# Reordering the first mixer layer of a one-core encoder kernel: q/k products, one output-gate tile and the gate logits ahead of the S5 input matrices

## What is computed

```
proj = xn @ w_in                       # 1024 -> 4 x 512: u, xm, v, o_pre
y_a = s5_group(u)                      # 32 groups x 16 channels, 64 complex states each
xc = silu(conv4(xm))                   # per head of 128
q, k = xc @ ml_w_q, xc @ ml_w_k        # 4 heads
gates = concat(q, k, v) @ ml_w_gates   # 8 logits: input and forget gate of 4 heads
h_t = rmsnorm(mlstm_chunkwise(q, k, v, gates))
y_b = sigmoid(o_pre) * h_t
out = concat(y_a, y_b) @ w_out
```

## Time and profile before

| | us |
|---|---|
| median of 3 runs | 1131.56 (1131.46 to 1132.12) |
| the profiled execution, its own time | 1132.59 |
| its span, first to last instruction | 1130.8 |
| PE busy | 1094.9 (97%) |
| PEld busy | 883.0 (78%) |
| DVE busy | 649.8 (57%) |
| ACT busy | 465.2 (41%) |
| POOL busy | 208.8 (18%), nearly all of it in the first 174 us |

### The profile page before, as it was taken

The page is one execution under the profiler, slowest core; times in us unless marked ns, Lnnn a source line. Parts: engine busy times, 40 slices in busy tenths (PEclk is TensorE's granted clock), DMA queues, the critical chain, the costliest instruction groups (busy, mean ns, idle before and its releaser), DMA issues.

```text
span 1130.8 us, 15508 instructions
## 1 busy us (share of the span) xinstructions
PE 1094.9 (97%) x5542; PEld 883.0 (78%) x5542; DVE 649.8 (57%) x871; ACT 465.2 (41%) x671; POOL 208.8 (18%) x312
## 2 busy tenths in 40 slices
PE   9969998999999999999999999999999999999997
PEld 7847656887888888888887777777888888888886
DVE  6798863556666666653333666266666666652323
ACT  6424553445434443432323365355434444432221
POOL 7998991020000000000000022030000000000000
PEclk9989998999999999999999999999999999999999
DMA  6641200422232222232333211032322223323222
GB/s 218 167 97 60 91 1 1 167 94 94 93 101 103 93 93 93 96 109 98 107 107 116 68 56 57 21 129 94 106 98 93 93 94 103 99 93 112 94 93 75
DMA packets 36491, 106.73 MB, mean 94 GB/s; under 512 B 7840, under 2 KB 10144, under 8 KB 36320
## 3 DMA queue, kind: packets, MB, share of 16 engines
q1 hardware_dynamic: 36448, 106.15, 28.7%
HBM read 101.55 MB, written 3.15 MB: 93 GB/s over the span
## 4 chain that ended last, share of the span: by engine, by line
PE 82%; DVE 4%; ACT 3%; issue 2%; POOL 0%; DVEq 0%; ACTq 0%; POOLq 0%
PE bank L1401 25%; PE bank L1403 25%; PE bank L1402 25%; PE bank L1743 1%; PE bank L1424 1%; ACT whi L645 1%; PE bank L1765 1%; PE bank L1563 1%; DVE h L1217 1%; PE bank L1596 0%; ACT sq L651 0%; PE bank L1543 0%; DVE xlo L949 0%; DVE wlo L943 0%; POOL ssum L435 0%
## 5 line engine op out<-in xcount | busy, mean ns | idle before, releaser
L1401 PE MATMUL bank<-xhi,whi 128*128 128x512 f32 x992 | 391.4, 395 | 7.6 <-DVE xlo L949 2.9
L1402 PE MATMUL bank<-xlo,whi 128*128 128x512 f32 x992 | 386.7, 390 | 0.0
L1403 PE MATMUL bank<-xhi,wlo 128*128 128x512 f32 x992 | 386.6, 390 | 0.0
L943 DVE TENSOR_TENSOR wlo<-raw,whi 128x1024 fp32r<-128x1024 f32 x177 | 223.5, 1263 | 269.0 <-ACT whi L645 268.4
L645 ACT ACTIVATE whi<-raw 128x1024 fp32r<-128x1024 f32 x177 | 187.1, 1058 | 378.3 <-PE bank L1403 350.6
L1401 PEld LDWEIGHTS bank<-xhi,whi 128*128 128x128 f32 x992 | 186.6, 188 | 52.1 <-issue 6.1
L1403 PEld LDWEIGHTS bank<-xhi,wlo 128*128 128x128 f32 x992 | 186.5, 188 | 39.4
L1402 PEld LDWEIGHTS bank<-xlo,whi 128*128 128x128 f32 x992 | 186.6, 188 | 38.6 <-issue 1.0
L1401 PE MATMUL bank<-ahi,whi 128*128 128x512 f32 (+1 forms) x374 | 142.5, 381 | 0.0
L1403 PE MATMUL bank<-ahi,wlo 128*128 128x512 f32 (+1 forms) x374 | 141.6, 379 | 0.0
L1402 PE MATMUL bank<-alo,whi 128*128 128x512 f32 (+1 forms) x374 | 140.4, 375 | 0.0
(11 more groups left out here) (236 smaller groups left out, 1097.4 us busy)
## 6 DMA issues: line engine op xcount, KB each, us to landing
raw<-wstream SPq DMA_DIRECT2D x177, 512.0 KB, 3.3
xin<-xT SPq DMA_DIRECT2D x8, 256.0 KB, 6.1
raw<-wstream SPq DMA_DIRECT2D x8, 256.0 KB, 5.3
h<-xT SPq DMA_DIRECT2D x1, 2048.0 KB, 8.4
outT<-outb SPq DMA_DIRECT2D x8, 256.0 KB, 2.2
u_scratch<-uperm SPq DMA_DIRECT2D x1, 1024.0 KB, 5.6
uc<-u_scratch SPq DMA_DIRECT2D x8, 128.0 KB, 5.2
bcp<-bc SPq DMA_DIRECT2D x1, 512.0 KB, 4.6
```

The lines of the kernel that those rows point to most:

```text
L943: V.tensor_tensor(wlo[:, t % RING, :], raw[:, t % RAWS, :], whi[:, t % RING, :].bitcast(f32), ALU.subtract).then_inc(lo_done, 1)
L1401: MM(dst, wh, rhi, start=start, stop=False)
L1402: MM(dst, wh, rlo, start=False, stop=False)
L1403: return MM(dst, wl, rhi, start=False, stop=stop)
```

## The change

- **PE**: the q/k products (now in banks 1, 2, 3, 0), the projection of tile 13 and the gate logits (now bank 7) stand ahead of the transposes of `gg`. The k products wait for a new semaphore `q_evac`.
- **ACT**: gets the copies of q (from DVE) and the two copies that build `cdiag` (from DVE), ahead of the k copies; the k copies and `split_hi` of tiles 16 and 17 stand ahead of the `m1` copies. Near the end of the mixer the gelu table is loaded ahead of `s5_output(2)`, and `head_hi(3)` stands ahead of the first gelu.
- **DVE**: `vT` copies 8 to 11 follow one another; `split_lo(13)` and `g_step` 1 to 3 follow; then it waits for `gates_ready`, makes `g8`, `split_lo` of 14, 15 and 16, `out_gate(0)` (with `split_lo(17)`), and only then `read_out` 0 to 3. It does the last three of the seven steps of the scan's last sweep, behind the loop over heads and ahead of `head_gate(3)`.
- **POOL**: clears `cdiag` at the start, and does four steps of the last sweep instead of seven.
- Buffers move (`m1re`, `m1im`, `qT`, `kT`, `g8`), two small ones are added.

```diff
@@ gpsimd @@
+        G.memset(cdiag[:, :, :, :, :], 0.0)
         G.memset(xs[:, :, :, 0:1], 0.0).then_inc(pads_set, 1)
...
+        G.memset(xs[:, 0, :, 0:1], 0.0).then_inc(carry_done, 1)
         a7, b7 = st1[:, :, 0:SUP - 1], st2[:, :, 0:SUP - 1]
-        for i in range(SUP - 1):
+        for i in range(4):
             axpy(XX[:, :, 1:, i], ...
@@ scalar, behind the split_hi of tile 15 @@
+        for f in range(2):
+            r = slice(STATE * f, STATE * f + STATE)
+            A(cdiag[r, :, :, f, :], bcp[r, 2:4, :].rearrange("p r (j i) -> p r j i", i=GCH),
+              ACT.Copy).then_inc(cdiag_set, 1)
+        for hd in range(HEADS):
+            act.wait_ge(qk_ready, hd + 1)
+            A(qT[:, hd, :], bank[QK_BANK[hd]][:, :], ACT.Copy).then_inc(q_evac, 1)
+        for hd in range(HEADS):
+            act.wait_ge(qk_ready, HEADS + hd + 1)
+            A(kT[:, hd, :], bank[QK_BANK[hd]][:, :], ACT.Copy).then_inc(k_evac, 1)
+        split_hi(T_QK + RING)
+        split_hi(T_O + RING)
         for b in range(8):
             act.wait_ge(m1_ready, b + 1)
...
         head_factor(HEADS - 1)
+        act.preload_act_table_set("gelu_apprx_tanh_and_others")
         s5_output(2)
+        head_hi(HEADS - 1)
         s5_gelu(0)
         s5_output(3)
-        head_hi(HEADS - 1)
         s5_gelu(1)
@@ vector @@
         for t in range(12):
-            if t:
-                wait_tile_used(dve, max(t, 3))
+            wait_tile_used(dve, max(t, 3))
+            if 0 < t < 9:
                 split_lo(t + RING)
...
-            if 8 <= t < 11:
-                g_step(t - 7)
...
+        dve.wait_ge(g0_done, 1)
+        dve.wait_ge(q_done, 1)
+        split_lo(T_QK + 1)
+        for step in range(1, 4):
+            g_step(step)
+        dve.wait_ge(gates_ready, 1)
+        V.tensor_scalar(g8[:, :], bank[7][0:104, :], col("bgate", 0, 104), None, ALU.add).then_inc(gates_copied, 1)
+        split_lo(T_QK + 2)
+        split_lo(T_QK + 3)
+        wait_tile_used(dve, T_QK)
+        split_lo(T_QK + RING)
+        out_gate(0)
         for step in range(3):
             read_out(step)
...
+        for i in range(4, n):
+            dve.wait_ge(carry_done, 1)
+            re, im = qk2[:, :, i:i + 1], aj2[:, :, i:i + 1]
+            steps.up(V.tensor_tensor(a7, re.to_broadcast([P, 2 * PAIRS, n]), XX[:, :, 0:n, SUP - 1], ALU.mult))
+            steps.up(V.tensor_tensor(b7[:, 0:PAIRS], im[:, 0:PAIRS].to_broadcast([P, PAIRS, n]),
+                                     X[1][:, :, 0:n, SUP - 1], ALU.mult))
+            steps.up(V.tensor_tensor(b7[:, PAIRS:], im[:, PAIRS:].to_broadcast([P, PAIRS, n]),
+                                     X[0][:, :, 0:n, SUP - 1], ALU.mult))
+            settle()
+            steps.up(V.tensor_tensor(a7, a7, b7, ALU.add))
+            settle()
+            V.tensor_tensor(XX[:, :, 1:, i], XX[:, :, 1:, i], a7, ALU.add).then_inc(sweep_done, 1)
         head_gate(HEADS - 1)
@@ tensor, behind the projection of tile 11 @@
+        for b in range(8):
+            hd = b % 4
+            if b < 4:
+                pe.wait_ge(out_freed, max(k + 1 for k in range(12) if IN_BANK[k] == QK_BANK[hd]))
+            else:
+                pe.wait_ge(q_evac, hd + 1)
+            block3(bank[QK_BANK[hd]][:, :], T_QK % RING, b, xchi[:, hd, :], xclo[:, hd, :], True,
+                   True).then_inc(qk_ready, 1)
+        pe.wait_ge(k_evac, 1)
+        project(T_O, O_O)
+        pe.wait_ge(k_evac, HEADS)
+        pe.wait_ge(rms_done, 1)
+        for k in range(12):
+            ...
+        ins.then_inc(gates_ready, 1)
...
         for b in range(8):
+            if b == 3:
+                pe.wait_ge(gates_copied, 1)
             if b >= 4:
                 pe.wait_ge(m1_copied, b - 3)
...
         pe.wait_ge(s5in_copied, 2)
         for hd in range(HEADS):      # transposes of vT, banks 5 to 7
...
         pe.wait_ge(scan_done, 1)
+        pe.wait_ge(sweep_done, SUP - 5)
```

More of the change, by code:

```diff
@@ L53 @@
 assert T_WO + KB == T_UP[1] and T_END % 2 == 1
-O_IN, O_QK, O_O, O_GLU, O_OUT = 0, 12, 16, 20, 24
-O_UP = [32, 102]
+O_IN, O_O, O_GLU, O_OUT = 0, 12, 16, 20
+O_UP = [28, 98]
 O_DN = [O_UP[0] + 2 * FJ, O_UP[1] + 2 * FJ]
@@ L61 @@
 RAWS, RING = 2, 4
-IN_BANK = (0, 1, 2, 3, 4, 5, 6, 0, 1, 2, 3, 0, 1, 2, 3, 0, 1, 2, 3, 0)
+IN_BANK = (0, 1, 2, 3, 4, 5, 6, 0, 1, 2, 3, 0, 1, 2, 3, 0)
+QK_BANK = (1, 2, 3, 0)
 COLS = {}
@@ L189, in build @@
     F4 = [P, 2, PAIRS, P]
-    (ff, gg, m1re, m1im, uc, uperm, xchi, xclo, sigo, xs, ksb) = plan(
-        ("ff", F4, f32), ("gg", F4, f32), ("m1re", F2, f32), ("m1im", F2, f32),
+    (ff, gg, qT, kT, uc, uperm, xchi, xclo, sigo, xs, ksb) = plan(
+        ("ff", F4, f32), ("gg", F4, f32), ("qT", [P, HEADS, SEQ], f32), ("kT", [P, HEADS, SEQ], f32),
         ("uc", [P, GROUPS, NCH], f32), ("uperm", [P, 4, SEQ], f32),
@@ L203, in build @@
     xin = at("xin", [P, KB, SEQ], m1_at)
-    qT = at("qT", [P, HEADS, SEQ], m1_at)
-    kT = at("kT", [P, HEADS, SEQ], m1_at + 8192)
+    m1re = at("m1re", F2, xc_at)
+    m1im = at("m1im", F2, xc_at + 8192)
     ga = at("ga", [P, 4, SEQ], m1_at)
@@ L291, in build @@
     x_back, cdiag_set = sem("x_back"), sem("cdiag_set")
-    g0_done, g_mid, q_done, k_evac, f_done = (sem(n) for n in ("g0_done", "g_mid", "q_done", "k_evac", "f_done"))
+    g0_done, g_mid, q_done, q_evac, k_evac, f_done = (sem(n) for n in (
+        "g0_done", "g_mid", "q_done", "q_evac", "k_evac", "f_done"))
     kt_copied, kt_ready = sem("kt_copied"), sem("kt_ready")
     c_negated, f_last = sem("c_negated"), sem("f_last")
+    carry_done, sweep_done = sem("carry_done"), sem("sweep_done")
     kdup_in = sem("kdup_in")
@@ L715, in _ @@
             ins.then_inc(s5in_copied, 1)
[L716 to L720, removed]
         for hd in range(HEADS):
@@ L1004, in read_out, with out_gate @@
             dve.wait_ge(f_done, s + 1)
+        def out_gate(m):
+            wait_tile_used(dve, T_O + m)
+            V.tensor_tensor(sigo[:, m, :], bank[IN_BANK[O_O + m]][:, :], rstd[:, :], ALU.mult).then_inc(out_freed, 1)
+            if m < 3:
+                split_lo(T_O + m + RING)
         def conv_lo(m):
@@ L1170, in _ @@
                 head_sum(hd - 1)
+        X = [xs[:, r, :, 1:NCH + 1].rearrange("p j (s i) -> p j s i", i=SUP) for r in range(2)]
+        XX = xs[:, :, :, 1:NCH + 1].rearrange("p r j (s i) -> p (r j) s i", i=SUP)
+        n = SUP - 1
+        a7, b7 = sv1[:, :, 0:n], sv2[:, :, 0:n]
+        for i in range(4, n):
[10 more added lines that the diff above has]
+            V.tensor_tensor(XX[:, :, 1:, i], XX[:, :, 1:, i], a7, ALU.add).then_inc(sweep_done, 1)
+            if i < n - 1:
+                dve.wait_ge(sweep_done, i - 3)
         head_gate(HEADS - 1)
@@ L1472, in _ @@
             ins.then_inc(s5in_ready, 1)
[L1474 to L1486, removed]
-        pe.wait_ge(s5in_copied, 2)
-        pe.wait_ge(k_evac, HEADS)
-        for k in range(12):
-            q = k % 4
-            ins = MM(bank[4][32 * q:32 * q + 8, :], cols("wg")[:, 8 * k:8 * k + 8],
-                     (qT, kT, vT)[k % 3][:, k // 3, :], start=k < 4, stop=k >= 8)
-        ins.then_inc(gates_ready, 1)
+        pe.wait_ge(s5in_copied, 2)
         for hd in range(HEADS):
```

39 lines of the change are left out of this document (10 added, 29 removed).

## The result

The changed kernel takes 1142.7 us (median of 4 runs, 1142.37 to 1144.31) against 1131.84 for the kernel before: ratio 1.0098, 95% interval 1.0081 to 1.0116. It is slower, as forecast, but by 10.9 us where 5.0 was forecast, and 0.9 us above the end of the range.

The account below looks back on a forecast made before the run. PE, busy 97% of the span, was taken as the bound. Terms 3.3 + 0.5 + 0.5 + 4.8 - 4.1 = +5.0 us on the median 1131.56 gave 1136.6 us, range 1131.8 to 1141.8.

Parts of the forecast that it names:

- The holes: Layer 0's mixer: PE's wait of 12.6 us becomes three, of 6.2, 6.5 and 2.1 us.
- Second stretch, to the `vT` transposes: From gate logits to vT transposes: PE waits 6.5 us for m1 copies, 2.1 for xs; loss 3.3 us at its end.
- milestone: Start of the vT transposes on PE in layer 0's mixer: forecast 114.5 against 111.16 before, 3.3 us lost.
- The third hole's clock: At the wait for xs copies: a clock drop there would cost 1 us more; 0.5 was taken.
- The heads: Between vT transposes and S5 output: POOL's later large scan steps slow DVE, +0.5 us, bounds -0.5 and 1.5.
- The scan and the sweep: At the S5 output: PE waits 4.8 us for DVE's three steps of 2.0 each, bounds 3.8 and 6.2.
- The end of the mixer: Ahead of the gated linear unit: the 2.75 us wait and its 1.4 us clock drop go, -4.1 us.
- The first: Rival at the second hole: tiles 16 and 17 don't hold ACT; 6.8 us less, 1129.8 us; chance 0.08.
- The steps on DVE were not hidden: Rival at the S5 output: DVE's three steps are hidden, the 4.8 us goes, 1131.8 us; chance 0.10.
- POOL was not last with four of them: Rival at the S5 output: POOL's scan ends last, PE waits 2.7 us more, 1139.3 us; chance 0.12.
- The change doesn't do what its order suggests: Rival: moved 13.9 us of work fill the hole, -12.6, and the end gives -4.1; about 1115 us; chance 0.02.
- The forecast's own range: Whole kernel time if the main forecast holds, not a rival: 1133.1 to 1141.5 us; chance 0.68.

Follow-up runs that it names:

- the fillers: Changed kernel plus 24 matrix products nobody reads in PE's second hole: 1140.06 us; with 24 more in the first hole too: 1138.52 us.
- the sweep alone: Kernel before, with only the last three steps of the scan's last sweep moved from POOL to DVE: 1139.11 us, ratio 1.0056.
- both holes closed: Changed kernel with low parts of tiles 14 and 15 ahead of DVE's gate wait, and ACT's high part of tile 15 behind its q/k copies: 1128.78 us.
- only ACT not held: Changed kernel with ACT's m1 copies moved ahead of its high parts of tiles 16 and 17: 1144.59 us, ratio 1.0112.
- splits ahead of the wait: Changed kernel with DVE's low parts of tiles 14 and 15 made ahead of its wait for the gate logits: 1132.18 us, ratio 1.0006.

## Why the prediction was wrong

The mechanism was right and a term was too small: the low clock behind the waits. I priced it for the first stretch of work behind each wait only, and at nothing behind the wait at the S5 output. Measured against that it cost 4.6 us more (0.5, 2.2, 1.1 and 0.8 below), of 6.7 that are missing. The next largest, 1.85, lies ahead of the first k product.

- **The holes (right).** Three holes at the places and with the releasers named: 6.24, 7.20 and 2.17 us, forecast 6.2, 6.5 and 2.1. The added wait for `gates_ready`, with splits, loads and `m1` copies behind it, is the cause; moving two splits ahead of it gave back 10.5 us. The rule of the Trainium skill that the prediction names (PSUM — Partial Sum Buffer, section "Engine vs sequencer instructions": these queues are strictly first in, first out) agrees with this trace: a ready bank waited from 98.2 to 106.23 on ACT, behind two splits that waited for their loads.
- **Second stretch, to the `vT` transposes (the step that failed, by size).** Forecast a loss of 3.3, milestone 114.5; measured 8.4, at 119.58. Of the 5.1 missing, 1.85 came in ahead of the first k product (84.65, forecast 82.8): DVE's list was 2.3 us later in this execution (`split_lo(12)` at 71.78 against 69.50), so that PE waited 1.79 for `xclo`, and tile 15 came late. 0.5 came by the four k products, which took 4.8 us, mostly at the low clock, where I took 4.3. 0.6 came by tile 17's load (the hole ended at 106.86, forecast 104.0, less the 2.3 that was late already). The largest, 2.2, was the small S5 products, from 111.22 to the `xs` copies at 117.46: 6.2 us, where I took 4.0 at the full clock. I had the clock fall in the hole and be back after the transposes; it stayed at 0.50 till 116.2.
- **The third hole's clock.** 0.5 taken, 1.6 measured (3.63 against 2.00). That the clock costs is shown by the fillers: 2.6 and 1.5 us given back by work that nobody reads. They don't show the whole 4.6: the fillers stand in two of the four places.
- **The heads.** Forecast +0.5, measured -0.5. A likely reason, not tested by itself: POOL's scan had moved out of DVE's way, not into it, since the `read_out` sums were done before it began. Half a microsecond is also within what two executions differ by.
- **The scan and the sweep (right in size, incomplete in cause).** A step on DVE takes 2.14 (taken 2.0, bounds 1.67 and 2.47), the wait is 5.3 (taken 4.8). That POOL's four steps were forecast to end at 178.6 and ended at 178.55 is luck: the scan started 5.2 us later than forecast, its steps up to the last sweep took 44.9 us and not 49.7, and the four took 13.9 and not 14.3. The first group behind the wait ran at the low clock, 0.8 more, which I had not priced. But "PE waits for DVE" is one of two reasons that each suffice here. Three steps behind the heads cost 5.3 also where the scan starts early (the sweep alone, both holes closed); and with POOL alone the scan's start, moved from 98.83 to 119.69 by the front, makes PE wait as long, and the time is the same.
- **The end of the mixer (right).** -4.0 in the ledger, -4.1 forecast, and 1127.86 by itself.
- **Rivals.** The first was priced wrongly even where its condition holds: I wrote that the chain from the milestone on is otherwise the same, and took -6.8. With only ACT not held the time stayed at 1144.6, since DVE's sums were the next bound; with the loads earlier too (splits ahead of the wait) it fell by 10.5. The steps on DVE were not hidden, and POOL was not last with four of them. The change doesn't do what its order suggests.
- **The sum.** The misses against +5.0 are +5.1 (milestone), +1.1 (clock), -1.0 (heads), +0.6 and +0.8 (S5 output) and +0.1 (end of the mixer), that is +6.7, and 5.0 + 6.7 = 11.7. The profiled execution lies 1.6 above its kernel's median and that of before 0.8 above its own, hence 10.9 in the medians. The forecast's own range was given up to 1141.5, but its high ends add up to 1131.56 + 10.3 = 1141.9; the measured 1142.7 lies above both.

What stays open: where the 1.85 us ahead of the first k product come from. At 41 us the DVE lists of the two kernels still agree (41.14 and 41.16), and they drift apart in the convolution beside POOL. In the ten experiments built on the changed kernel, with the same code up to there, `split_lo(12)` started anywhere from 69.32 to 72.99, in the two built on the kernel before at 72.40 and 73.21. Where it started by 70.61 PE had no wait for `xclo`; where it started at 71.78 or later, one of 1.8 to 2.3 (in the changed kernel and its variants). So the changed kernel need not be the reason: dates of two single executions can differ here by up to 3.7 us in the same code.

## What to carry to other kernels

When work is moved into a hole, a wait that is added on an in-order engine delays everything listed behind it, loads and other engines' copies too: put what is ready (here two splits of 2.35 us) ahead of the wait, and long independent work into the idle time that the wait makes. When an estimate says that a hole closes, look for the second bound and for what the earlier date triggers: here it started GpSimd's scan earlier, beside VectorE's sums, and a gain of 11 us at one date was gone at the next. When work is divided between two engines, time each engine's part while the other is at work: a step of DVE's took 4.0 us and not 2.14. And price a hole in TensorE with the slow clock behind it, over all the small work until the granted clock is seen to return, not over the first group alone.

## What the runs showed of the hardware

The granted clock stayed at 0.50 for 13.6 us (102.6 to 116.2), while PE worked from 106.86 on for all but 0.7 us, on transposes and on the small S5 products; I had expected it back with the first of these products. In the kernel before, behind the hole of 12.6 us, it was back at 90.0, after 3.8 us of the same transposes. With 24 products of 128x512 in the second hole of the changed kernel it stayed at 1.00 throughout in one profiled execution (one filler), and in another it fell to 0.50 behind them (two fillers). What decides between these is not shown. An operation of VectorE on 224 elements takes 0.39 us when they are neighbours and 0.55 when they stand apart in `xs`; my bounds for a step came from the rows on either side. Beside GpSimd's steps of the same sweep the two took 0.76 and 1.10.
